# Products of the next heads cut into pieces between the units of two attentions

## The chip, the cores and the metric

The kernel runs on one core of one Trainium2 chip. The metric is the device time of one execution in microseconds (us). Its engines, as the profile names them: PE is TensorE's matmuls, PEld its weight loads, DVE is VectorE, ACT is ScalarE, POOL is GpSimd and SP is SyncE.

## What is computed

A network of two blocks over 512 tokens of width 1024, all in float32. The first block has four layers: a latent attention, a sliding attention, a sparse attention and a latent attention again, each normed, shifted and scaled by a modulation. The second has a hybrid of attention and state space, a short convolution and two gated feed-forward layers. The change touches the two middle layers of the first block:

```python
def swa_mixer(h, positions, w_in, sinks, w_out):
    q, k, v, gate = jnp.split(h @ w_in, ...)            # 16 heads of 64, 2 key heads
    q, k = rope(q), rope(k)
    o = banded_attention(q, k, v, 128, 128, sinks)      # window of 128
    return (o * jax.nn.silu(gate)) @ w_out

def nsa_mixer(h, positions, w_in, cmp_pos, w_cmp_k1, w_cmp_k2, w_cmp_v1, w_cmp_v2, w_out):
    q, k_cmp, v_cmp, k_slc, v_slc, k_win, v_win, g_branch, gate = jnp.split(h @ w_in, ...)
    ...                                                 # 16 heads of 64, 4 key heads
    o = g[..., 0:1] * o_c + g[..., 1:2] * o_s + g[..., 2:3] * o_w
    return (o * jax.nn.silu(gate)) @ w_out
```

`o_c` is attention over 31 compressed blocks, `o_s` over chosen blocks (with 512 tokens all are chosen, so it is causal attention), `o_w` over a window of 512.

## The kernel before

Each engine has its own program, written out by hand, and semaphores join them. An attention runs over units. In the sparse layer (`nsa_units`) a pair of heads has 17: unit 0 is the compressed branch of both heads, units 1 to 8 are the branch of chosen blocks (4 blocks of 128 queries, both heads of each in turn), units 9 to 16 the window; a unit is 128, 256, 384 or 512 keys wide by its query block. There are 8 pairs, so 136 units. In the sliding layer (`swa_units`) a pair has 4 units, one for each query block with both heads.

TensorE's `attend` goes through the steps. At step s it first does what `inserts` holds for s, then the scores of unit s, then it waits for ScalarE's copy of the turned probabilities of unit s-3 and multiplies them with the values (`values`, L1237 and L1226, in the sliding layer L1111; in branches 1 and 2 only after the second head, with both heads' blocks), then it waits for VectorE's normalised probabilities of unit s-2 and turns them (`turn_blocks`, L894) into the one bank PB. VectorE does at step s the row maxima of unit s (L2434; for the compressed branch the three operations L2427 to L2429) and the normalisation of unit s-1 (L2648, L2649). Where VectorE's `inserts` has an entry for the step, the normalisation comes first, then the insert, then the maxima; else the maxima come first. ScalarE does at step s its insert, the copy of the turned unit s-2 (L1754), and the exponential of unit s (L1743).

The inserts make what the next pair needs. `query` and `gate` are products of 8 matmuls of 512 columns (L726), `turn` is one matmul with a rotation table (L726, `psum<-raw,cst`), after which VectorE's `rotate` finishes the rotary embedding. After even pairs the next key head's values are made (`value_tile`, L753), after odd pairs its keys (`key_tile`) and their turn (`key_turn`): ScalarE's part of that waits for VectorE's rotation and makes two copies (L1970, L1971). All go through two PSUM banks by turns: `next_tile` waits until the tile before the last is free, `evacuated` until a tile has been read. Weights come through a ring of two slots (`open_slot`); the load of a slot is issued when the first matmul of the slot before it has run. Query and gate of a pair share a slot. A matmul in float32 is two records in the trace.

`mod_columns(3)` at step 34 sums the columns of GpSimd's job (48 records, L781). `drain_inserts` puts parts of the output projection (L920) into the last steps. The steps at which the products stood, on all three engines: query 2, turn 4, gate 6, next 9, next turn 11 in the sparse layer; query 1, turn 2, gate 3 in the sliding one.

Of the kernel before, what the change touches and what calls it, by code (L numbers as in the profile page):

```python
# [185 lines left out]
NEVER = 3.0e38  # L186
MLA_STEPS = {1: "queries", 2: "keys", 4: "gate 0", 6: "gate 1", 7: "values"}
SWA_STEPS = {1: "query", 2: "turn", 3: "gate"}
NSA_STEPS = {2: "query", 4: "turn", 6: "gate", 9: "next", 11: "next turn"}


def causal_blocks(j):
# [39 lines left out]
def build(nc, A, out, tables, const):  # L232

    ctx = ExitStack()
    with ctx:
# [457 lines left out]
        def _(pe):  # L693
# [382 lines left out]
            def query_tiles(raw_tiles, slots_of):  # L1076
# [10 lines left out]
                    rotated(raw[:, 0, :])  # L1087
                return query, gate, turn

            def swa():  # L1090
                query, gate, turn = query_tiles({}, {})

# [31 lines left out]
                turn(0)  # L1124
                inserts = {}
                for pair in range(7):
                    for at, name in SWA_STEPS.items():
                        part = {"query": query, "gate": gate, "turn": turn}[name]
                        inserts[4 * pair + at] = [lambda part=part, pair=pair: part(pair + 1)]
                attend(swa_units(), scores, turn_blocks, values, inserts={**inserts, **drain_inserts(swa_units())})  # L1130

            def nsa():
# [47 lines left out]
                def value_tile(kv):  # L1180
                    value_tiles[kv] = tokens_tile(open_slot(2), P, range(TT), True)

                key_tile(0)
                slot = open_slot(3)
# [54 lines left out]
                                          stop=(u["branch"] == 2 and i == len(u["blocks"]) - 1), skip_group_check=True)  # L1239
                    return m  # L1240

                inserts = {}
                for pair in range(7):
                    kv = pair // 2 + 1
                    base = 17 * pair
                    inserts[base + 2] = [lambda pair=pair: query(pair + 1)]
                    inserts[base + 4] = [lambda pair=pair: turn(pair + 1)]
                    inserts[base + 6] = [lambda pair=pair: gate(pair + 1)]
                    if pair < 6 and pair % 2 == 0:
                        inserts[base + 9] = [lambda kv=kv: value_tile(kv)]  # L1250
                    if pair < 6 and pair % 2:
                        inserts[base + 9] = [lambda kv=kv: key_tile(kv)]
                        inserts[base + 11] = [lambda kv=kv: key_turn(kv)]
                inserts[17 * 2] = [lambda: mod_columns(3)]
# [426 lines left out]
        def _(act):  # L1681
# [244 lines left out]
            def nsa():  # L1926
# [82 lines left out]
                attend(nsa_units(), -1.0, inserts=inserts)  # L2009

# [238 lines left out]
        def _(dve):  # L2249
# [356 lines left out]
            def nsa():  # L2606
# [78 lines left out]
                for pair in range(7):  # L2685
                    kv = pair // 2 + 1
                    base = 17 * pair
                    inserts[base + 2] = [lambda pair=pair: query(pair + 1)]
                    inserts[base + 4] = [lambda pair=pair: turn(pair + 1)]
                    inserts[base + 6] = [lambda pair=pair: gate(pair + 1)]  # L2690
                    if pair < 6 and pair % 2 == 0:
                        inserts[base + 9] = [lambda kv=kv: value_tile(kv)]
                    if pair < 6 and pair % 2:
                        inserts[base + 9] = [lambda kv=kv: key_tile(kv)]
                        inserts[base + 11] = [lambda kv=kv: key_turn(kv)]
# [540 lines left out]
```

## Time and profile before

| | |
|---|---|
| median of 3 runs | 2867.77 us (2866.61 to 2868.32) |
| the profiled execution | 2861.63 us, its span 2859.8 us |
| mean granted TensorE clock in it | 0.978 |
| TensorE (PE) busy | 2705.7 us, 95% of the span |
| VectorE, ScalarE, GpSimd busy | 1296.1, 655.7, 1072.3 us |
| units of the sliding attention | 367 to 538 us of the span |
| units of the sparse attention | 683 to 1052 us of the span |

The profile is of one execution. A busy TensorE is counted with each matmul's full length, while the next one may start before it ends. In a timeline, idle time and what ended it stand in brackets behind an instruction.

### The profile page before, as it was taken

What the parts mean: (1) busy time and instruction counts of PE and PEld (TensorE: products, weight loads), DVE (VectorE), ACT (ScalarE), POOL (GpSimd) and SP (SyncE); (2) the same over time, 40 slices, a digit from 0 to 9 for tenths busy, and PEclk for the clock granted to TensorE, in tenths of its full rate; (3) what the DMA queues carried; (4) which work ended last, traced back from release to release, by engine and by line L of the source; (5) the groups of instructions that cost most, each with busy time, mean ns of one, the idle gap of its engine ahead of it and who ended that gap; (6) DMA issues with size and microseconds to landing.
All of it is one profiled execution on the core that took longest, in us unless ns stands there. A gap on an engine that the chain in (4) does not pass through costs nothing.

```text
span 2859.8 us, 32196 instructions
## 1 busy us (share of the span) xinstructions
PE 2705.7 (95%) x11791; PEld 1767.7 (62%) x11791; DVE 1296.1 (45%) x2667; ACT 655.7 (23%) x1575; POOL 1072.3 (37%) x574
## 2 busy tenths in 40 slices
PE   6799999998999999999998889899999999999997
PEld 5366544465555554555545665778887444888886
DVE  7133355333655552333555674443554222433554
ACT  2133123232333342322113621111101001111101
POOL 4785188048583003860584001880000880000000
PEclk7899999999999999999999999999999999999999
DMA  7342343145242103331442002442222542222222
GB/s 243 105 133 86 99 130 111 59 122 148 67 119 59 37 30 123 111 98 62 116 134 58 1 16 81 154 155 83 85 92 87 162 159 74 74 83 82 86 91 70
DMA packets 245112, 277.81 MB, mean 97 GB/s; under 512 B 41427, under 2 KB 217824, under 8 KB 244864
## 3 DMA queue, kind: packets, MB, share of 16 engines
q1 hardware_dynamic: 216000, 175.03, 20.2%
q0 software_dynamic: 28224, 100.86, 11.4%
q8 instruction: 78, 1.28, 0.2%
q10 hardware_dynamic: 768, 0.30, 0.0%
q14 instruction: 42, 0.34, 0.0%
HBM read 274.06 MB, written 2.10 MB: 97 GB/s over the span
## 4 chain that ended last, share of the span: by engine, by line
PE 84%; DVE 4%; DMA 3%; ACT 3%; issue 3%; POOL 1%; SPq 1%; DVEq 0%; ACTq 0%; POOLq 0%
PE psum L726 27%; PE psum L1523 25%; PE psum L920 12%; PE psum L894 3%; PE psum L1219 2%; PE psum L781 2%; PE psum L1237 1%; PE psum L906 1%; DMA ring<-in_ffn_w_gate 1%; PE psum L1059 1%; PE psum L1060 1%; PE psum L753 1%; PE psum L1354 1%; DMA ring<-in_ffn_w_up 1%; POOL ada_ring L668 1%
## 5 line engine op out<-in xcount | busy, mean ns | idle before, releaser
L726 PE MATMUL psum<-h,ring 128*128 128x512 f32 (+1 forms) x1776 | 758.9, 585 | 15.3 <-ACT arena L1704 4.7
L656 POOL DMA_DIRECT2D ada_ring<-in_ada_w x192 | 114.7, 597 | 1266.0 <-DVEq L2336 796.0
L726 PEld LDWEIGHTS psum<-h,ring 128*128 128x128 f32 x1776 | 335.7, 192 | 399.5 <-issue 381.9
L668 POOL TENSOR_SCALAR ada_ring<-ada_ring,cond 128x1024 f32<-128x1024 f32 x168 | 480.5, 2860 | 8.4 <-POOL ada_sum L672 2.1
L672 POOL TENSOR_TENSOR ada_sum<-ada_sum,ada_ring 128x1024 f32<-128x1024 f32 x168 | 398.6, 2373 | 14.9
L920 PE MATMUL psum<-og,ring 128*128 128x512 f32 x768 | 333.3, 593 | 0.3
L1523 PE MATMUL psum<-og,arena 128*128 128x256 f32 x1152 | 258.6, 379 | 1.7 <-ACT probs L2160 1.7
L920 PEld LDWEIGHTS psum<-og,ring 128*128 128x128 f32 x768 | 144.5, 190 | 179.1 <-issue 179.1
L1523 PEld LDWEIGHTS psum<-og,arena 128*128 128x128 f32 x1152 | 218.7, 190 | 32.1 <-issue 2.4
L1523 PE MATMUL psum<-h,ring 128*128 128x256 f32 x768 | 177.7, 382 | 1.6 <-DVE mods L2334 0.9
L1754 ACT ACTIVATE probsT<-psum 128x128 f32<-128x128 f32 (+3 forms) x232 | 104.3, 450 | 293.9 <-PE psum L894 293.2
L1523 PEld LDWEIGHTS psum<-h,ring 128*128 128x128 f32 x768 | 145.7, 191 | 25.9 <-ACT h L1719 5.1
L1787 ACT ACTIVATE sq<-x 128x512 f32<-128x512 f32 x63 | 39.7, 630 | 424.7 <-DVE x L2500 228.5
L2160 ACT ACTIVATE probs<-psum 128x256 f32<-128x256 f32 x132 | 50.7, 384 | 373.1 <-PE psum L1523 373.1
L3036 DVE SCALAR_TENSOR_TENSOR x<-psum,mods,x 128x256 f32<-128x256 f32 x168 | 81.1, 483 | 112.1 <-PE psum L1523 110.8
L894 PE MATMUL psum<-cst,arena 128*128 128x128 f32 x608 | 112.3, 286 | 20.2 <-ACT probsT L1754 10.8
L2500 DVE SCALAR_TENSOR_TENSOR x<-psum,mods,x 128x512 f32<-128x512 f32 x48 | 36.0, 751 | 204.3 <-PE psum L920 203.9
L1743 ACT ACTIVATE psum<-psum,neg_max 128x256 f32<-128x256 f32 (+3 forms) x256 | 122.1, 477 | 26.4 <-DVE neg_max L2434 26.1
L2434 DVE CUSTOM_DVE_ANT_0 psum<-psum,cst 128x128 f32<-128x128 f32 (+1 forms) x192 | 94.5, 499 | 72.4 <-PE psum L1060 33.6
L1704 ACT ACTIVATE arena<-psum 128x512 f32<-128x512 f32 (+4 forms) x100 | 55.0, 557 | 281.2 <-PE psum L726 228.0
L1523 PE MATMUL psum<-og,ring 128*128 128x256 f32 x400 | 98.9, 391 | 17.8 <-DVE arena L3010 17.8
L1523 PE MATMUL psum<-h,arena 128*128 128x256 f32 x480 | 113.4, 379 | 0.0
(383 smaller groups left out, 3578.0 us busy)
## 6 DMA issues: line engine op xcount, KB each, us to landing
ada_ring<-in_ada_w POOLq DMA_DIRECT2D x192, 512.0 KB, 4.1
ring<-in_ffn_w_gate SPq DMA_DIRECT2D x22, 1024.0 KB, 5.4
ring<-in_ffn_w_up SPq DMA_DIRECT2D x22, 1024.0 KB, 5.3
ring<-in_ffn_w_down SPq DMA_DIRECT2D x16, 1024.0 KB, 5.1
ring<-in_sc_w_in SPq DMA_DIRECT2D x12, 1024.0 KB, 6.0
ring<-in_mla_w_in SPq DMA_DIRECT2D x10, 1024.0 KB, 5.4
ring<-in_mla_w_out SPq DMA_DIRECT2D x8, 1024.0 KB, 5.2
ring<-in_swa_w_in SPq DMA_DIRECT2D x16, 512.0 KB, 5.4
```

The costliest lines, as they stand in the source:

```text
L656: pool.dma_start(ada_ring[:, i % 2, :], w[k * P:(k + 1) * P, first(part)]).then_inc(arrived[i % 2], n.give(f"ada_in{i % 2}", 16))
L668: step = nc.gpsimd.tensor_scalar(piece, ada_ring[:, i % 2, :], c, None, ALU.mult)
L672: step = nc.gpsimd.tensor_tensor(total, total, piece, ALU.add)
L726: m = pe.matmul(tile.at[:, part], lhs(k), rhs(k), start=(k == 0), stop=(k == K - 1))
L781: m = pe.matmul(tile.at[:, c:c + width], ada_sum[:, c * P:(c + 1) * P], ones[:, 0:width], start=True, stop=True)
L894: m = pe.transpose(bank[:, i * P:(i + 1) * P], p[:, block_at:block_at + P], ident)
L920: m = pe.matmul(out_tiles[c].at, w8(out_slots[0], P * (c % 2))(k), og[:, k * T:(k + 1) * T], start=(k == 0), stop=(k == KT - 1))
L1523: last = pe.matmul(out, weights[:, k, :], moving[:, k, :], start=begins and k == 0, stop=True, skip_group_check=True)
L1743: e = nc.scalar.activation(scored, scored, ACT.Exp, bias=neg_max[:, step % 4, g:g + 1], scale=scale, accum_out=row_sum[:, step % 4, g:g + 1])
L1754: c = nc.scalar.activation(probsT[:, i % 2, 0:w], PB[:, 0:w], ACT.Copy)
L2434: last = nc.vector.tensor_tensor_reduce(s[:, at:at + w], s[:, at:at + w], mask(u), -scale, floor, ALU.add, ALU.min, neg_max[:, b, g:g + 1])
L3036: nc.vector.scalar_tensor_tensor(xq, bank, scales[q], xq, ALU.mult, ALU.add).then_inc(S[told], n.give(told))
```

## The change

In the sparse layer TensorE's query, gate and next products are cut into pieces of one to three matmuls (`NSA_PIECES`), one piece a step, so that the last piece stands at the step of `NSA_STEPS`. Query: steps 0, 1, 2. Turn: 4. Gate: 4 to 8. Next keys or values: 9 to 13. Next turn: 15. VectorE's and ScalarE's parts stand at the steps of the last pieces, so gate goes from 6 to 8, next from 9 to 13, next turn from 11 to 15. In the sliding layer TensorE's query is cut four and four over steps 0 and 1, its gate four and four over steps 2 and 3; the other engines' steps stay. `pieces` and `value_pieces` are new functions; they issue the same matmuls in the same order within a product.

```diff
-NSA_STEPS = {2: "query", 4: "turn", 6: "gate", 9: "next", 11: "next turn"}
+NSA_STEPS = {2: "query", 4: "turn", 8: "gate", 13: "next", 15: "next turn"}
+NSA_PIECES = {"query": (3, 3, 2), "gate": (1, 1, 2, 2, 2), "next": (2, 2, 1, 1, 2)}
...
+            def pieces(sizes, weights, slot_of=None):
+                made, out, at = {}, [], 0
+                def piece(first, size):
+                    if first == 0:
+                        if slot_of is not None:
+                            made["slot"] = slot_of()
+                        made["tile"] = next_tile()
+                    for k in range(first, first + size):
+                        m = pe.matmul(made["tile"].at, weights(made)(k), h_lat(k), start=(k == 0), stop=(k == KT - 1))
+                        if k == 0 and slot_of is not None:
+                            m.then_inc(S["slot_begun"], n.give("slot_begun"))
+                    if first + size == KT:
+                        m.then_inc(S["tile_done"], 1)
+                for size in sizes:
+                    out.append(lambda at=at, size=size: piece(at, size))
+                    at += size
+                return out, made
+
+            def value_pieces(sizes, tiles, kv):
+                made, out, at = {}, [], 0
+                def piece(first, size):
+                    if first == 0:
+                        made["slot"] = open_slot(2)
+                        tiles[kv] = next_tile()
+                    for i in range(first, first + size):
+                        j, half = i // 2, i % 2
+                        for k in range(4 * half, 4 * half + 4):
+                            m = pe.matmul(tiles[kv].at[:, j * P:(j + 1) * P], h[:, k, j * P:(j + 1) * P],
+                                          w8(made["slot"], 0)(k), start=(k == 0), stop=(k == KT - 1))
...
             def swa():
...
-                    for at, name in SWA_STEPS.items():
-                        part = {"query": query, "gate": gate, "turn": turn}[name]
-                        inserts[4 * pair + at] = [lambda part=part, pair=pair: part(pair + 1)]
+                    base = 4 * pair
+                    asked, made = pieces((4, 4), lambda m: w8(m["slot"], 0), lambda: open_slot(2))
+                    gated, _ = pieces((4, 4), lambda _, made=made: w8(made["slot"], P))
+                    def turned(made=made):
+                        evacuated(made["tile"])
+                        rotated(raw[:, 0, :])
+                    for at, part in enumerate([[asked[0]], [asked[1]], [turned, gated[0]], [gated[1]]]):
+                        inserts[base + at] = part
...
             def nsa():
...
-                inserts = {}
+                inserts = {step: [] for step in range(17 * 8)}
+                inserts[17 * 2].append(lambda: mod_columns(3))
+                def spread_over(last, parts, base):
+                    for i, part in enumerate(parts):
+                        inserts[base + last + 1 - len(parts) + i].append(part)
...
-                    inserts[base + 2] = [lambda pair=pair: query(pair + 1)]
-                    inserts[base + 4] = [lambda pair=pair: turn(pair + 1)]
-                    inserts[base + 6] = [lambda pair=pair: gate(pair + 1)]
+                    spread_over(at["query"], asked, base)
+                    spread_over(at["turn"], [turned], base)
+                    spread_over(at["gate"], gated, base)
                     if pair < 6 and pair % 2 == 0:
-                        inserts[base + 9] = [lambda kv=kv: value_tile(kv)]
+                        spread_over(at["next"], value_pieces(NSA_PIECES["next"], value_tiles, kv), base)
                     if pair < 6 and pair % 2:
-                        inserts[base + 9] = [lambda kv=kv: key_tile(kv)]
-                        inserts[base + 11] = [lambda kv=kv: key_turn(kv)]
+                        keyed, key_made = pieces(NSA_PIECES["next"], lambda m: w8(m["slot"], 0), lambda: open_slot(2))
+                        def keys_turned(key_made=key_made):
+                            evacuated(key_made["tile"])
+                            rotated(raw[:, 0, :])
+                        spread_over(at["next"], keyed, base)
+                        spread_over(at["next turn"], [keys_turned], base)
...
 # on ScalarE and on VectorE alike
-                    inserts[base + 6] = [lambda pair=pair: gate(pair + 1)]
+                    inserts[base + 8] = [lambda pair=pair: gate(pair + 1)]
                     if pair < 6 and pair % 2 == 0:
-                        inserts[base + 9] = [lambda kv=kv: value_tile(kv)]
+                        inserts[base + 13] = [lambda kv=kv: value_tile(kv)]
                     if pair < 6 and pair % 2:
-                        inserts[base + 9] = [lambda kv=kv: key_tile(kv)]
-                        inserts[base + 11] = [lambda kv=kv: key_turn(kv)]
+                        inserts[base + 13] = [lambda kv=kv: key_tile(kv)]
+                        inserts[base + 15] = [lambda kv=kv: key_turn(kv)]
```

## Rows read from the trace of the kernel before

**Rows 1.** Stretches of both attentions and of one clock dip (busy by engine, clock, DMA).

```profile
367.00:526.00 159.00, 156.22 (x595) 74.29 (x596) 92.86 (x281) 56.47 (x214) 111.23 (x58) 1.00 0.38 109
683.00:1052.00 369.00, 346.12 (x1907) 205.70 (x1908) 214.19 (x629) 139.82 (x421) 150.97 (x78) 0.99 0.24 69
869.00:875.00 6.00, 4.29 (x14) 2.29 (x15) 3.29 (x12) 3.76 (x12) 5.57 (x4) 0.72 0.31 86
```

**Rows 2.** TensorE's waits, 684 to 1052: us in total, times, longest.

```profile
PE psum L894 <- ACT probsT L1754: 10.8, 12, 2.2
PE psum L894 <- DVE arena L2649: 7.1, 6, 1.2
PE psum L1237 <- ACT probsT L1754: 3.0, 9, 0.6
```

**Rows 3.** TensorE's timeline, pair 1 of the sparse attention: start, us, instruction, count, idle before.

```profile
728.20 0.39 PE L1219 MATMUL psum<-arena 128*128 128x128 f32 x2
729.78 0.63 PE L894 MATMUL psum<-cst,arena 128*128 128x128 f32 x4 [1.20 <-DVE arena L2649]
...
743.26 7.03 PE L726 MATMUL psum<-h,ring 128*128 128x512 f32 x16
750.13 0.81 PE L1219 MATMUL psum<-arena 128*128 128x384 f32 x2
...
750.99 1.02 PE L1219 MATMUL psum<-arena 128*128 128x512 f32 x2
751.95 0.66 PE L1237 MATMUL psum<-probsT,arena 128*64 128x128 f32 x8
...
752.92 1.02 PE L1219 MATMUL psum<-arena 128*128 128x512 f32 x2
754.01 0.52 PE L894 MATMUL psum<-cst,arena 128*128 128x128 f32 x3
...
763.70 0.66 PE L894 MATMUL psum<-cst,arena 128*128 128x128 f32 x4 [0.46 <-ACT probsT L1754]
764.19 1.02 PE L726 MATMUL psum<-raw,cst 128*128 128x512 f32 x2
...
766.77 0.60 PE L1219 MATMUL psum<-arena 128*128 128x256 f32 x2
769.58 0.33 PE L894 MATMUL psum<-cst,arena 128*128 128x128 f32 x1 [2.21 <-ACT probsT L1754]
...
771.22 0.81 PE L1219 MATMUL psum<-arena 128*128 128x384 f32 x2
772.17 0.41 PE L894 MATMUL psum<-cst,arena 128*128 128x128 f32 x2
```

**Rows 4.** TensorE's timeline: a value product in sliding pair 1, one in sparse pair 0.

```profile
387.85 0.66 PE L1111 MATMUL psum<-probsT,arena 128*64 128x128 f32 x8 [0.25 <-ACT probsT L1754]
...
718.41 1.09 PE L1237 MATMUL psum<-probsT,arena 128*64 128x128 f32 x16 [0.25 <-ACT probsT L1754]
```

**Rows 5.** TensorE's timeline, last steps of the sliding attention.

```profile
530.88 2.74 PE L920 MATMUL psum<-og,ring 128*128 128x512 f32 x6
533.55 0.66 PE L1111 MATMUL psum<-probsT,arena 128*64 128x128 f32 x8
```

**Rows 6.** Timeline of VectorE and TensorE where the sparse units start.

```profile
681.15 0.69 DVE L2408 SCALAR_TENSOR_TENSOR arena<-arena,psum 128x512 f32<-128x512 f32 x1 [6.18 <-ACT arena L1726]
...
683.28 1.10 PE L1215 MATMUL psum<-arena 128*128 128x64 f32 x8 [2.02 <-DVEq L2389]
```

**Rows 7.** ScalarE's timeline at the key turn of pair 1.

```profile
768.10 0.63 ACT L1970 ACTIVATE arena<-arena 64x512 f32<-64x512 f32 x1 [2.76 <-DVEq L2389]
...
769.27 0.25 ACT L1754 ACTIVATE probsT<-psum 128x128 f32<-128x128 f32 x1
```

**Rows 8.** Loads of queries and gates: count, KB, us to landing.

```profile
ring<-in_nsa_w_in SPq DMA_DIRECT2D x16, 512.0 KB, 5.1
```

**Rows 9.** GpSimd's timeline after the column sums of step 34.

```profile
781.77 0.61 POOL L656 DMA_DIRECT2D ada_ring<-in_ada_w  x1 [26.90 <-DVE gains L2310]
```

More of the change, by code:

```diff
@@ L1088, in query_tiles @@
                 return query, gate, turn
+            def pieces(sizes, weights, slot_of=None):
[26 more added lines that the diff above has]
+                                          w8(made["slot"], 0)(k), start=(k == 0), stop=(k == KT - 1))
+                            if i == 0 and k == 0:
+                                m.then_inc(S["slot_begun"], n.give("slot_begun"))
+                    if first + size == 2 * TT:
+                        m.then_inc(S["tile_done"], 1)
+                for size in sizes:
+                    out.append(lambda at=at, size=size: piece(at, size))
+                    at += size
+                return out
             def swa():
@@ L1178, in key_turn @@
                     rotated(raw[:, 0, :])
-                def value_tile(kv):
-                    value_tiles[kv] = tokens_tile(open_slot(2), P, range(TT), True)
                 key_tile(0)
@@ L1245, in nsa, with turned @@
                     base = 17 * pair
-                    inserts[base + 2] = [lambda pair=pair: query(pair + 1)]
-                    inserts[base + 4] = [lambda pair=pair: turn(pair + 1)]
-                    inserts[base + 6] = [lambda pair=pair: gate(pair + 1)]
+                    at = {name: step for step, name in NSA_STEPS.items()}
+                    asked, made = pieces(NSA_PIECES["query"], lambda m: w8(m["slot"], 0), lambda: open_slot(2))
+                    gated, _ = pieces(NSA_PIECES["gate"], lambda _, made=made: w8(made["slot"], P))
+                    def turned(made=made):
+                        evacuated(made["tile"])
+                        rotated(raw[:, 0, :])
+                    spread_over(at["query"], asked, base)
+                    spread_over(at["turn"], [turned], base)
+                    spread_over(at["gate"], gated, base)
                     if pair < 6 and pair % 2 == 0:
-                        inserts[base + 9] = [lambda kv=kv: value_tile(kv)]
+                        spread_over(at["next"], value_pieces(NSA_PIECES["next"], value_tiles, kv), base)
                     if pair < 6 and pair % 2:
-                        inserts[base + 9] = [lambda kv=kv: key_tile(kv)]
-                        inserts[base + 11] = [lambda kv=kv: key_turn(kv)]
-                inserts[17 * 2] = [lambda: mod_columns(3)]
+                        keyed, key_made = pieces(NSA_PIECES["next"], lambda m: w8(m["slot"], 0), lambda: open_slot(2))
+                        def keys_turned(key_made=key_made):
+                            evacuated(key_made["tile"])
+                            rotated(raw[:, 0, :])
+                        spread_over(at["next"], keyed, base)
+                        spread_over(at["next turn"], [keys_turned], base)
                 attend(nsa_units(), scores, turn_blocks, values, inserts={**inserts, **drain_inserts(nsa_units())})
@@ L2689, in nsa @@
                     inserts[base + 4] = [lambda pair=pair: turn(pair + 1)]
-                    inserts[base + 6] = [lambda pair=pair: gate(pair + 1)]
+                    inserts[base + 8] = [lambda pair=pair: gate(pair + 1)]
                     if pair < 6 and pair % 2 == 0:
-                        inserts[base + 9] = [lambda kv=kv: value_tile(kv)]
+                        inserts[base + 13] = [lambda kv=kv: value_tile(kv)]
                     if pair < 6 and pair % 2:
-                        inserts[base + 9] = [lambda kv=kv: key_tile(kv)]
-                        inserts[base + 11] = [lambda kv=kv: key_turn(kv)]
+                        inserts[base + 13] = [lambda kv=kv: key_tile(kv)]
+                        inserts[base + 15] = [lambda kv=kv: key_turn(kv)]
                 inserts[17 * 2] = [lambda: mod_columns(3, col("norm_g", 24, 8))]
```

## The prediction

> **What bounds the kernel now.** I read the page first (the table above): TensorE is busy 95% of the span, so the time can only fall by work that leaves TensorE (none does: the change moves products and removes none) or by stalls that leave it. Then the two stages that the change touches, as stretches: in the sliding attention TensorE is busy 156.2 of 159 us, in the sparse attention 346.1 of 369 us, at granted clocks of 1.00 and 0.99 [rows 1]. So the sparse stage holds some 23 us of idle time and the sliding one 3. Then who ended these waits: ScalarE's copies of turned probabilities and VectorE's normalised ones, 10.8, 7.1 and 3.0, together 20.9 us in 27 waits, none over 2.2 us [rows 2]. They are latencies of the hand-over between the engines, not a full engine: VectorE is busy 214 and ScalarE 140 of the 369 us [rows 1]. Last the timeline of one pair of heads [rows 3], which shows where in the 17 steps they stand.
>
> How [rows 3] must be read: a recorded matmul is longer than the time until the next may start. A product of 16 records starts at 743.26 and the scores after it at 750.13: 6.87 us, 0.43 for each record of 512 columns, recorded as 0.59; in proportion 0.32, 0.22 and 0.11 us for 384, 256 and 128 columns. A true stall is thus the start minus the end by these spacings, some 0.16 us more than the idle time in brackets, and there are stalls with no bracket. The stalls of a pair, its branch-0 unit being step 0:
> - step 1: scores at 728.20 take 0.22, the turning starts at 729.78: 1.36 us. VectorE first does the three maxima operations of the compressed branch, then the normalisation that is waited for. Six times: pairs 1, 3, 5 and 6 as here, pair 4 with 0.14 less, pair 2 only 0.62 (idle 0.46): 7.3 us together.
> - step 8: 752.92 + 0.86 = 753.78, next start 754.01: 0.23 us, in seven pairs.
> - step 10: idle 0.46 before 763.70, so 0.62 us, in eight pairs; it is the copy of four turned blocks that must leave the one bank.
> - step 11 of pairs with no key turn there: idle 0.25 at 718.41, some 0.32 us over what such a start costs anyway (0.09) [rows 4].
> - step 12 of pairs 1, 3 and 5: scores at 766.77 take 0.44, the turning starts at 769.58: 2.37 us.
> - step 14: 771.22 + 0.65 = 771.87, next start 772.17: 0.30 us, in eight pairs.
>
> **What the change does, part by part.** *Cutting products up.* Per pair the query goes 3, 3 and 2 matmuls at steps 0 to 2 (it was 8 at step 2), the gate 1, 1, 2, 2, 2 at steps 4 to 8 (8 at step 6), the next keys or values in five pieces at steps 9 to 13 (all at 9); the key turn goes from 11 to 15. That adds 2 x 7 + 4 x 7 + 4 x 6 = 66 interruptions of an accumulation in the sparse stage and 14 in the sliding one, 80 together. Their price: a turning of four blocks starts at 763.70 and a product with the rotation table at 764.19, four spacings of 0.11 and 0.05 later; at 750.13 the scores follow a product at its own spacing [rows 3]. The output projection's accumulation is already interrupted in the sliding stage's last steps: six records start at 530.88, the values at 533.55, which is 6 x 0.43 + 0.09 [rows 5], and 0.10 is what a start of values costs behind scores too (750.99 + 0.86, then 751.95 [rows 3]). I take 0 per interruption; the upper end is 0.1 us, 8 us in all; no row suggests a gain.
>
> *Cover.* One matmul is two records, 0.86 us; pieces of 1, 2 and 3 are 0.86, 1.71 and 2.57 us. Each stall is a chain on other engines that runs on while TensorE works, so a piece between its start and its end takes it away up to the piece's length. Step 1 gets 2.57 us between scores(0) and the awaited turning, against 1.36: gone in pairs 1 to 6, 7.3 us. Step 8 gets 1.71 against 0.23: seven times, 1.6 us. Step 10 gets 1.71 or so against 0.62 in the six pairs with a next product: 3.7 us. Step 11, 0.86 against 0.32 in pairs 0, 2, 4: 1.0 us. Step 14 gets no piece, but VectorE now has an entry at step 13 and so normalises unit 12 before the maxima of 13, and not after: the 0.30 goes in six pairs, 1.7 us (bounds 0 and 1.7). Pair 7 has no products and keeps its stalls; pair 6 has no next product and keeps steps 9 to 11 (some 1.1 us of idle time).
>
> *Start of each attention.* Scores of pair 0 wait 2.02 us of idle time, 2.17 by spacing, for VectorE's rotation. Now the first piece stands ahead of them. It needs the bank that VectorE's gate product frees at 681.15 + 0.69 = 681.84, 0.73 us after the rotating matmul is through (683.28 - 2.17); it ends at 681.95 + 2.57 = 684.5, after the rotation. Scores then start at 684.5, where before scores and the same 2.57 us would have been through 683.28 + 2.57 = 685.85: 1.3 us saved [rows 6]. The sliding stage starts in the same way (the same 2.02 us of idle time): 1.3 us more.
>
> *The key turn.* ScalarE's part of it waits for VectorE's rotation, then makes two copies, and only then copies the turned block that TensorE waits for: it stands idle 2.76 us until 768.10, copies to 769.27, then takes the block, and TensorE goes on at 769.58 [rows 3, 7]. From 764.14, the end of the turning before it, the chain is 5.4 us, and TensorE has 3.0 us of work beside it. Moved to step 15 the chain has the same members. From the turning of step 14: copy 0.5 and exp 0.7, normalising 0.8, rotation 2.1, copies 1.2, block 0.4, with hand-overs some 5.9 us; TensorE has rotation 0.86, scores 0.86, values 0.66, turning 0.33, scores 0.86, together 3.6. The stall moves to step 16 with 2.3 us; if VectorE is still behind from taking the keys at step 13, 2.6. No piece stands at step 16, and those of the next step 0 come behind the wait. So 2.4 three times is given back as 2.4 or 2.5: cost 0.3 us in all (bounds: 3 us better, 2 us worse). Queued behind it is the turning of step 16; the next scores come 2.6 us later, which hides the late exp and normalisation.
>
> *What gets less cover.* In pair 0 the compressed unit's turning at step 2 has 1.7 + 0.2 us after scores(1), and VectorE takes maxima 0.3 and weighing 1.8 first: 0.7 us new. Pair 6's gate now ends at step 8, VectorE's and ScalarE's work on it stands right before the uncovered steps 9 and 10: 0.3 us new. Elsewhere the chains (1.5 to 3.9 us) lie under 4 to 6 us of TensorE work. VectorE's operations are sometimes stretched beside GpSimd; I leave up to 2 us for that.
>
> *Sliding attention.* The query goes 4 and 4 at steps 0 and 1, the gate 4 and 4 at 2 and 3. At each step 0 a value product waits 0.25 us (387.85) [rows 4], 0.32 by spacing; six of these steps now get 3.43 us ahead of them, 1.9 us, and one turning of pair 0 saves 0.2. VectorE's and ScalarE's steps don't move there.
>
> *Loads.* A slot's load starts with the first matmul of the slot before. The query is now opened two steps earlier, but still eight steps after its load starts, and the loads land in 5.1 us [rows 8]; TensorE's waits name none [rows 2]. GpSimd's job that the column sums of step 34 read was through at 754.9, for GpSimd then stands idle 26.90 us for what comes of these sums [rows 9], so they may come 10 us earlier.
>
> **The sum.** Sparse: 7.3 + 1.6 + 3.7 + 1.0 + 1.7 + 1.3 - 0.3 - 0.7 - 0.3 = 15.3 us. Sliding: 1.3 + 1.9 + 0.2 = 3.4. Together 18.7 us. The profiled execution took 2861.6 (span 2859.8), it would take 2843; the median of the runs is 6.1 higher, and there I take off the same: 2867.8 - 18.7 = 2849.
>
> **The clock.** Two dips fall in the sparse stage, each 6 us at 0.72 on average, so 1.7 us lost, and both follow a key-turn stall [rows 1] (the other at 968 to 974); pair 1 has the same stall and no dip. As that stall stays, I keep both; 3.4 us is the most that can be won. The Trainium skill ("TensorE: Matmul & The Clock Gate", A second HAM failure mode: psum-queue depth-cycling) says that matmul groups which go round the PSUM banks leave TensorE idle so briefly and so often that its clock swings between the two levels. By that rule the cut products would cost clock. This trace disagrees: the sliding stage changes bank every 1 to 3 us and is granted 1.00.
>
> **Rivals.**
> 1. *As forecast*, 12 to 23 us saved: 0.70.
> 2. *The stalls come back elsewhere*: the chain of each unit is late at the small pieces (0.86 us) or behind the key turn, or interruptions cost near 0.1 us. Half the gain, 6 to 12 us: about 2858. For it: steps 14 to 16 have no piece. Against: pair 7, with no pieces at all, has only 3.3 us of idle time. 0.16.
> 3. *Nothing to be measured*: the piece boundaries cost 0.2 us, as each start of a value product costs 0.09 and some of the compressed branch's 0.2: 80 x 0.2 = 16, leaving 3 us: about 2865. 0.08.
> 4. *Slower*: an interrupted accumulation costs a start of its own. From 0.29 us per interruption, 80 of which are 23 us, the kernel is over 0.2% slower; at 0.35 it is 28 - 18.7 = 9 us slower, 2877. Against it: [rows 5]. 0.02.
> 5. *Clock swings*, the skill's rule as a mechanism of this kernel: a dip in each of 14 pairs instead of 2, 12 x 1.7 = 20 us: 2869, no change. Against: the sliding stage's 1.00 with two dozen changes of bank a pair [rows 1]. 0.04 (of which half slower).
>
> **Numbers.** What a measurement tells from no change is 0.2%, 5.7 us. Faster: 0.86 (cases 1 and 2); within: 0.10; slower: 0.04. The range must hold 8 in 10: case 1 from 23 us (both dips and part of the key turn gone: 2844) and case 2 to about 9 us: 2859.
>
> **What would show it.** Right: TensorE's waits in the sparse stage fall from 21 us to some 10, namely three of 2.2 to 2.5 us behind the key turn, now at step 16, and the rest in pairs 6 and 7; no 1.20 at step 1 except in pair 7; the stage, 369 us, is some 15 shorter with the same busy time; spacing at piece ends 0.11 and 0.43. The start waits of 2.02 shrink to about 0.7 or turn into one for the bank. Wrong: spacings over 0.5 us at piece ends (cases 3, 4), new waits at steps 4 to 8 or of more than 3 us at 16 (case 2), a granted clock below 0.98 (case 5). It would also be wrong if the key turn's stall vanished: then some 7 us more.

## The result, and the profile after

The changed kernel took 2846.48 us (median of 6 runs, 2840.47 to 2853.9), the kernel before 2867.35 us (6 runs, 2858.96 to 2869.29). The ratio is 0.993 with an interval of 0.9912 to 0.9948: some 20 us less, between 15 and 25. The forecast was 2849 us and 18.7 us less.

The profiled execution took 2844.35 us, 17.3 less than the one before; its span is 2842.5. On the page TensorE is busy 95% of the span as before (2705.7 us then), and its granted clock has the same tenths:

```profile
PE 2699.3 (95%) x11791; PEld 1768.6 (62%) x11791; DVE 1314.0 (46%) x2667; ACT 659.5 (23%) x1575; POOL 1069.4 (38%) x574
...
PEclk7899999999999999999999999999999999999999
```

The windows of the two attentions, from the rotating matmul ahead of the first unit to where the output projection goes on after the last values (before: 364.29 to 538.75 and 680.25 to 1051.77), and of two clock dips (columns as in [rows 1]):

```profile
363.46:538.84 175.38, 170.74 (x655) 80.87 (x653) 114.82 (x301) 64.43 (x234) 112.91 (x58) 0.99 0.35 105
677.67:1031.20 353.53, 340.48 (x1909) 206.12 (x1908) 215.01 (x630) 143.96 (x423) 155.73 (x81) 1.00 0.26 74
527.00:533.00 6.00, 4.87 (x17) 2.60 (x18) 2.86 (x12) 2.47 (x8) 0.00 (x0) 0.72 0.09 16
766.00:772.00 6.00, 4.35 (x24) 4.35 (x25) 3.40 (x8) 3.42 (x8) 0.00 (x0) 0.72 0.01 1
```

The sparse attention is 353.5 us long where it was 371.5: 18.0 less. One dip of the clock lies in it (at 768, behind the key turn of pair 1) where there were two, which is 1.7 us of that; the stalls are the other 16.3. The sliding attention is 175.4 us where it was 174.5, with a dip at 529 that was not there (1.7 us): at equal clock it is 0.8 less, and 3.4 were forecast. What lies outside both made 0.2 us: 0.8 less ahead of them, 2.7 less between them, where the clock dips cost 5.1 us before and 1.7 now, and 3.3 more behind them, in code that the change doesn't touch. Single executions differ by that much.

TensorE's waits of the sparse stage, which answer to [rows 2] (L895 turns blocks, L1285 multiplies with values, L1101 is a piece of a product, L2714 normalises):

```profile
PE psum L895 <- ACT probsT L1819: 7.0, 4, 2.2
PE psum L1285 <- ACT probsT L1819: 2.3, 6, 0.6
PE psum L895 <- DVE arena L2714: 1.8, 2, 1.2
PE psum L1101 <- DVE arena L2473: 0.7, 1, 0.7
PE psum L895 <- DVE arena L2723: 0.5, 1, 0.5
```

Together these are 11.6 us beside the 0.7 at the first piece; before it was 20.9. The timeline shows where, by the readings of [rows 3, 6]:

```profile
677.67 1.02 PE L727 MATMUL psum<-raw,cst 128*128 128x512 f32 x2
679.42 2.81 PE L1101 MATMUL psum<-h,ring 128*128 128x512 f32 x6 [0.72 <-DVE arena L2473]
682.07 1.00 PE L1263 MATMUL psum<-arena 128*128 128x64 f32 x8
...
688.38 0.44 PE L895 MATMUL psum<-cst,arena 128*128 128x128 f32 x2 [0.52 <-DVE arena L2723]
...
728.59 0.39 PE L1267 MATMUL psum<-arena 128*128 128x128 f32 x2
728.81 0.60 PE L895 MATMUL psum<-cst,arena 128*128 128x128 f32 x4
...
764.44 1.02 PE L1267 MATMUL psum<-arena 128*128 128x512 f32 x2
767.65 0.56 PE L895 MATMUL psum<-cst,arena 128*128 128x128 f32 x3 [2.19 <-ACT probsT L1819]
```

The first piece waits 0.72 us for the bank of the gate tile and the first scores start at 682.07; those wait for nothing. In pair 1 the turning follows the scores of step 1 at 0.22 us, the bare spacing, where it stood 1.36 us. At step 16 it stands 2.19 us by the row, 767.65 - 764.44 - 0.86 = 2.35 by spacing. ScalarE's rows are those of [rows 7], four steps later:

```profile
765.95 0.63 ACT L2035 ACTIVATE arena<-arena 64x512 f32<-64x512 f32 x1 [3.02 <-DVEq L2454]
...
767.13 0.47 ACT L1819 ACTIVATE probsT<-psum 128x384 f32<-128x384 f32 x1
```

In the sliding stage the 0.25 us waits of [rows 4] are gone from pairs 1 to 6 and the 2.02 us at its start are 0.72. But the first row here is new: before, TensorE waited 0.5 us once ahead of the rotating matmul (L727), for the query to be taken:

```profile
PE psum L727 <- DVE tmp L2441: 2.0, 3, 0.9
PE psum L1156 <- ACT probsT L1819: 0.9, 2, 0.7
```

The reason is on VectorE. It has the same 301 instructions and is busy 114.8 us, not 99.9. One line makes the difference, the sum of `row_sum` and `sink_exp`, 128x2 elements. Its row before:

```profile
L2448 DVE TENSOR_TENSOR row_sum<-row_sum,sink_exp 128x2 f32<-128x2 f32 x32 | 13.6, 426 | 28.0 <-ACT psum L1743 27.9
```

and after:

```profile
L2513 DVE TENSOR_TENSOR row_sum<-row_sum,sink_exp 128x2 f32<-128x2 f32 x32 | 30.2, 944 | 24.1 <-ACT psum L1808 24.0
```

From 426 to 944 ns on average with single ones of 2351 ns, as long as GpSimd's sums take. It is not so in every execution, as the experiments show below. The timeline at pair 1 (GpSimd, VectorE and TensorE) shows what is behind it:

```profile
389.82 2.34 POOL L673 TENSOR_TENSOR ada_sum<-ada_sum,ada_ring 128x1024 f32<-128x1024 f32 x1
...
389.83 2.35 DVE L2513 TENSOR_TENSOR row_sum<-row_sum,sink_exp 128x2 f32<-128x2 f32 x1
...
393.21 1.46 DVE L2513 TENSOR_TENSOR row_sum<-row_sum,sink_exp 128x2 f32<-128x2 f32 x1
...
393.69 1.02 PE L1144 MATMUL psum<-arena 128*128 128x512 f32 x2
...
395.42 0.68 DVE L2440 COPY raw<-psum 128x512 f32<-128x512 f32 x1
...
396.76 0.70 PE L727 MATMUL psum<-raw,cst 128*128 128x512 f32 x1 [0.87 <-DVE tmp L2441]
```

The query is through at 393.7 us, but VectorE starts to take it at 395.42, behind two normalisations whose sums took 2.35 and 1.46 us, and TensorE's rotating matmul waits 0.87 us. The first of these sums starts 0.01 us behind a sum of GpSimd and ends with it. The second (393.21 to 394.67) ends with no instruction of GpSimd; what stretched it isn't shown.

### The profile page after: what moved, and what is told of

Its sections match the earlier page's. It is cut to its first block, busy times and chain, and to the rows that moved or that the text cites. A ratio compares the mean times of both kernels' runs of the same rounds, so it can differ in the third digit from the quotient of the medians.

```text
span 2842.5 us, 32196 instructions
## 1 busy us (share of the span) xinstructions
PE 2699.3 (95%) x11791; PEld 1768.6 (62%) x11791; DVE 1314.0 (46%) x2667; ACT 659.5 (23%) x1575; POOL 1069.4 (38%) x574
## 4 chain that ended last, share of the span: by engine, by line
PE 86%; DVE 4%; DMA 3%; ACT 2%; issue 2%; POOL 1%; SPq 1%; DVEq 0%; ACTq 0%; POOLq 0%
PE psum L1588 27%; PE psum L727 20%; PE psum L921 12%; PE psum L1101 7%; PE psum L895 3%; PE psum L1267 2%; PE psum L782 2%; PE psum L1285 1%; PE psum L907 1%; PE psum L1060 1%; PE psum L1061 1%; PE psum L1419 1%; PE psum L1123 1%; DMA ring<-in_ffn_w_gate 1%; POOL ada_ring L669 1%
## 5 line engine op out<-in xcount | busy, mean ns | idle before, releaser
L657 POOL DMA_DIRECT2D ada_ring<-in_ada_w x192 | 114.8, 598 | 1251.9 <-DVEq L2401 803.6
L727 PE MATMUL psum<-h,ring 128*128 128x512 f32 (+1 forms) x1280 | 538.9, 580 | 16.2 <-DVE arena L2345 4.7
L727 PEld LDWEIGHTS psum<-h,ring 128*128 128x128 f32 x1280 | 243.1, 192 | 295.4 <-issue 277.0
L1101 PE MATMUL psum<-h,ring 128*128 128x512 f32 x496 | 229.4, 593 | 1.4 <-DVE arena L2473 1.4
L1101 PEld LDWEIGHTS psum<-h,ring 128*128 128x128 f32 x496 | 87.8, 191 | 81.8 <-issue 81.0
L895 PE MATMUL psum<-cst,arena 128*128 128x128 f32 x608 | 110.9, 284 | 10.6 <-ACT probsT L1819 7.0
```

The lines of the kernel that those rows point to most:

```text
L657: pool.dma_start(ada_ring[:, i % 2, :], w[k * P:(k + 1) * P, first(part)]).then_inc(arrived[i % 2], n.give(f"ada_in{i % 2}", 16))
L727: m = pe.matmul(tile.at[:, part], lhs(k), rhs(k), start=(k == 0), stop=(k == K - 1))
L895: m = pe.transpose(bank[:, i * P:(i + 1) * P], p[:, block_at:block_at + P], ident)
L1101: m = pe.matmul(made["tile"].at, weights(made)(k), h_lat(k), start=(k == 0), stop=(k == KT - 1))
```

## The experiments

Times of a kernel come with the ratio to the kernel before on the same chip. Stage lengths and stalls are read from one profiled execution of each; the sparse stage is given from its first scores to its last values (368.3 us before, 348.9 in the changed kernel), and a stall by spacing. In the changed kernel the query's first piece, 2.57 us, stands ahead of the first scores and so outside this length; before, the whole query lay inside. The lengths therefore compare kernels that have this piece, and the 18.0 us above compare the change with the kernel before.

**The two layers apart.** One kernel has the sliding layer's edit alone, one the sparse layer's alone; the other layer's code is that of before.

> The sliding layer's cut alone, the sparse layer as before. My theory (cover of stalls at each step 0 and at the start): 3.4 us faster than before, so 2864, within 0.2% of it; in the profile the waits of 0.25 us at step 0 of pairs 1 to 6 are gone and the 2.02 us at the start has become 0.7. Rival (the sliding layer brings nothing, its products only go elsewhere): the same waits at other steps, 2867. Rival (an interruption costs 0.3 us or more): 14 of them, slower by 4.

2866.69 us against 2866.48, ratio 0.9987 (0.997 to 1.0004): no gain that can be told from none. The waits of 0.25 us are gone, and 2.04 us stand at one rotating matmul of pair 0, with a clock dip right behind it (376 to 380, 1.7 us). The rival that stalls change place is nearer than mine.

> The sparse layer's part alone, the sliding layer as before. My theory: 15 to 17 us faster than before, about 2851, with three waits of 2.2 us left at step 16 of pairs 1, 3 and 5. Rival (the two layers share the gain evenly): 2857.

2844.13 us, ratio 0.9915 (0.989 to 0.9939). The whole measured gain is here, with a stage of 350.3 us and two clock dips in it. The interval, 17 to 32 us, lies at and above my 15 to 17. The three waits of 2.2 us at step 16 are there as said.

**Moved and not cut.**

```diff
-NSA_PIECES = {"query": (3, 3, 2), "gate": (1, 1, 2, 2, 2), "next": (2, 2, 1, 1, 2)}
+NSA_PIECES = {"query": (8,), "gate": (8,), "next": (8,)}
```

> The steps of the sparse layer moved as in the change (gate 8, next 13, key turn 15), but each product in one piece of 8, and the sliding layer as before. My theory (cutting is what pays, since a cover is worth something only at the step where a chain runs out): the stalls of step 1 stay (7.3 us), those of 8 and 14 go (3.3 us), and steps 6, 9, 10 and 11 lose the cover they had, some 6 to 7 us, so 3 us slower than before, 2870, within 0.2%. Rival (the gain comes from the later steps and the earlier normalisation, not from the cutting): 10 us or more faster, 2855.

2879.9 us, ratio 1.005 (1.0036 to 1.0063): 14 us slower than before. The moves alone cost, and the rival that they are the gain is out. My 3 us were too few by a stall that the kernel before never shows, since its gate stood on it: behind the rotation of step 4, VectorE is late with unit 4, and the turning of step 6 waits. The scores at 744.47 take 0.65, the turning starts at 746.92, 1.80 us later, in seven pairs, 12.6 us:

```profile
744.47 0.81 PE L1261 MATMUL psum<-arena 128*128 128x384 f32 x2
746.92 0.41 PE L895 MATMUL psum<-cst,arena 128*128 128x128 f32 x2 [1.64 <-DVE arena L2708]
...
PE psum L895 <- DVE arena L2708: 21.6, 19, 1.6
```

**Is an interruption free?** Each piece of the changed kernel is halved, and the second half goes behind the scores.

```diff
+                        piece(at, size - size // 2)
+                        if size // 2:
+                            behind.append(lambda: piece(at + size - size // 2, size // 2))
...
```

> The changed kernel, but of every piece of 2, 3 or 4 matmuls the later half (rounded down) is put behind the scores of its step: some 88 interruptions more, the same work in each step. My theory (an interruption costs nothing): as the changed kernel within 2 us, 2846 to 2849, spacings 0.43 and 0.11 at the new ends. Rival (an interruption costs 0.1 us, and the change would have won 8 us more without them): 9 us slower than the changed kernel, 2856.

2846.19 us, ratio 0.9924 (0.9902 to 0.9946), as the changed kernel. In the timeline a piece (L1105), the scores (L1279), the other half and the values follow one another at 0.87, 0.22, 0.86 + 0.09 us:

```profile
732.35 0.60 PE L899 MATMUL psum<-cst,arena 128*128 128x128 f32 x4
732.78 1.02 PE L1105 MATMUL psum<-h,ring 128*128 128x512 f32 x2
733.65 0.38 PE L1279 MATMUL psum<-arena 128*128 128x128 f32 x2
733.87 1.02 PE L1105 MATMUL psum<-h,ring 128*128 128x512 f32 x2
734.82 1.09 PE L1297 MATMUL psum<-probsT,arena 128*64 128x128 f32 x16
```

The 88 more interruptions show no cost in the times of the runs. By their intervals alone up to some 0.07 us each could hide there; it is the spacings that show the bare rate. In the profile, the sliding stage is 1.8 us longer at equal clock, with waits at seven rotating matmuls, since the query's last half now comes behind the scores. The sparse stage is 3.3 us longer: the key turn's three stalls are 2.99 us and not 2.35, pair 6 stands 0.7 longer at step 10, both because the last half ends later; that leaves under 1 us for the 60 interruptions there.

**The key turn.** ScalarE's part goes behind the copy that TensorE waits for. VectorE's stays at 15.

```diff
-                        inserts[base + 15] = [lambda kv=kv: key_turn(kv)]
+                        inserts[base + 16] = [lambda kv=kv: key_turn(kv)]
```

> The changed kernel with one edit: ScalarE's part of the key turn (wait for the rotation, two copies) stands at its step 16 and not 15, so behind the copy of the turned unit 13 and the exponential of 15. My theory (the stall of 2.35 us at step 16 is that copy, queued behind a wait for VectorE's rotation): the three stalls go, 7 us less than the changed kernel, about 2840; at most 1 us comes back at the next pair's first steps. Rival (VectorE is late itself: behind the rotation stand the maxima and normalisation of 15, so the wait only changes its name): within 2 us of the changed kernel, with a wait for VectorE at step 16 or 0.

2840.23 us, ratio 0.9902 (0.9884 to 0.9919), 6 us less than the changed kernel, whose interval overlaps. The profile is clearer: the stage is 342.1 us, 6.8 less, of which 1.7 is the clock dip of the changed kernel that has no counterpart here, and the turning of step 16 follows its scores at the bare 0.86 us: three stalls of 2.35 us are gone. Of these, 1.5 us of idle time came back at the first scores of pairs 4 and 6 (L1263), which now wait for the copies themselves:

```profile
766.28 1.02 PE L1267 MATMUL psum<-arena 128*128 128x512 f32 x2
767.14 0.49 PE L895 MATMUL psum<-cst,arena 128*128 128x128 f32 x3
...
PE psum L1263 <- ACT arena L2036: 1.5, 2, 0.7
```

**Few pieces.** Two pieces a product; the query at 1 and 2, the gate at 7 and 8, the next one at 9 and 10.

```diff
+NSA_PIECES = {"query": (4, 4), "gate": (4, 4), "next": (4, 4)}
...
-                        spread_over(at["next"], keyed, base)
+                        spread_over(at["next"] - 3, keyed, base)
...
```

> The changed kernel with two pieces of 4 for each product of the sparse layer instead of three or five: query at steps 1 and 2, gate at 7 and 8, keys or values at 9 and 10; all later steps of the other engines as in the change. My theory (what counts is that some piece stands at a step where a chain runs out): step 1, 8, 9 and 10 stay covered; step 11 loses its cover (0.32 us in six pairs, 1.9 us), step 12 0.1, and behind the query's rotation at step 4 nothing stands at 5 and 6, where the uncut gate's absence cost 1.8 us in seven pairs in the kernel with moved, uncut products: 12.6 us. Sum 15 us slower than the changed kernel, about 2861. Rival (the number of pieces matters, small ones being better as such): the 15 us would be spread over all steps and not stand at step 6.

2869.32 us, ratio 1.0007 (0.9994 to 1.002): all of the gain is lost, 23 us against the changed kernel where I had said 15. Step 6 stands 1.80 us in each of seven pairs again, step 11 0.32 in all. Not foreseen: 0.76 us ahead of each key turn, since no piece stands at 13 while VectorE takes the keys, 0.64 more at the three stalls of step 16 and 0.25 in the even pairs, 1.2 us at the start, where no piece stands at step 0 now (scores wait 2.02 us again), and three clock dips in the stage, one of them double: 13.6 us at the lower level, so 6.8 us lost where the one dip of the changed kernel costs 1.7.

```profile
PE psum L895 <- DVE arena L2714: 13.3, 9, 1.6
PE psum L895 <- ACT probsT L1819: 8.9, 4, 2.8
```

Nearly the same number of pieces, better placed: the gate's two at steps 5 and 6, the query's two kept, the next product in three (3, 3, 2) at 9, 10 and 11.

```diff
+NSA_PIECES = {"query": (4, 4), "gate": (4, 4), "next": (3, 3, 2)}
...
-                    spread_over(at["gate"], gated, base)
+                    spread_over(at["gate"] - 2, gated, base)
...
```

> As the kernel with pieces of four, other steps: gate 4 and 4 at steps 5 and 6 (not 7 and 8), next product 3, 3, 2 at 9, 10, 11; what the other engines do stands at 8, 13 and 15 as in the change. My theory (a piece is worth something where a chain runs out, and behind the query's rotation that is step 6): the 1.8 us at step 6 of seven pairs and the 0.32 at step 11 go, 0.23 at step 8 comes, so some 13 us less than with pieces of four, about 2855; against the changed kernel it keeps what stands at 8, 14 and 16. Rival (pieces must be small): no better than pieces of four, 2869.

2855.3 us, ratio 0.9967 (0.9953 to 0.9981): 14 us less by the medians than the pieces of four before it, as said (11 by the ratios). Step 6 is free of stalls in the seven pairs. That small pieces are worth something as such is out; the place decides. It is still 9 us above the changed kernel. What it lacks to it is the start (2.02 us, for step 0 has no piece), the 0.76 us ahead of each key turn, step 16 (2.98 us three times, 0.25 in the even pairs), 1.1 more at step 10 of pair 6 and 0.11 at step 8. Step 14, where I had expected a stall, has none in pairs 0 to 5.

**The sliding layer.** The rotating matmul and the gate's first piece stand behind the scores of step 2.

> The changed kernel, but in the sliding layer the rotating matmul and the gate's first piece stand behind the scores of step 2 and not ahead of them. My theory (the new waits ahead of the rotating matmul, 0.7 to 1.05 us in pairs 0, 1, 3 and 5, are VectorE's taking of the query, which now runs behind a normalisation that the query's first piece has delayed): scores of 0.86 us cover most of them, the sliding stage is 1.5 to 2.3 us shorter at equal clock. Rival (the wait is for the bank of the tile, however late): it stays in full.

One run: 2844.0 us. The stage, from the rotating matmul to the last values, takes 170.1 us; it took 174.3 before and 175.2 (173.5 without the dip) in the changed kernel. The waits ahead of the rotating matmul are gone, and what is left is the 0.72 us for the bank at the start and the waits of the last pair's drain. The sum's operations, 682 ns on average here, no longer reach TensorE. At equal clock that is 3.4 us less than the changed kernel's profile, more than I had said; but that profile is one with long sums, as the table below shows, and against the best one of the same sliding code it is 0.7.

And the sum itself, in the changed kernel:

```diff
-                        settle(nc.vector.tensor_tensor(row_sum[:, b, 0:G], row_sum[:, b, 0:G], sink_exp[:, b, 0:G],
-                                                       ALU.add))
+                        for g in range(G):
+                            added = nc.vector.tensor_scalar(row_sum[:, b, g:g + 1], row_sum[:, b, g:g + 1],
+                                                            sink_exp[:, b, g:g + 1], None, ALU.add)
+                        settle(added)
```

> The changed kernel; in the sliding layer VectorE's sum of row_sum and sink_exp (128x2, both in SBUF, 32 times) is two operations of 128x1 with sink_exp as a column scalar. Its mean grew from 426 to 944 ns with the change, 16.6 us in all, with single ones of up to 2351 ns, which is as long as a sum of GpSimd. My theory (it waits for GpSimd's operation, and that wait stands ahead of the taking of the query): the two operations take about 0.15 us each, VectorE's busy time in the sliding stage falls by some 20 us, the new waits ahead of the rotating matmul shrink from 2.0 us of idle time to under 0.8, and the sliding stage is 1.5 to 2 us shorter. Rival (the late taking is from the order normalisation, then query, and not from GpSimd): VectorE's busy time falls, the waits ahead of the rotating matmul stay.

2844.18 us, ratio 0.9923 (0.9896 to 0.995): not told apart by the runs. By the profile: twice as many operations, 209 ns each (202 to 215), 10.7 us in place of 30.2; TensorE waits 0.5 us for the query as before the change, and the stage is 171.2 us.

```profile
L2514 DVE TENSOR_SCALAR row_sum<-row_sum,sink_exp 128x1 f32<-128x1 f32 x64 | 10.7, 209 | 27.9 <-ACT psum L1808 27.9
...
PE psum L727 <- DVE tmp L2441: 0.5, 1, 0.5
```

That alone doesn't show what the sum costs the change, for several of the other kernels have the very same sliding code as the changed one, and their profiled executions differ. Line, mean of the 128x2 sum, TensorE's waits at the rotating matmul, and the stage to the last values, 1.7 us a clock dip taken off:

| kernel | sum, ns | waits, us | stage, us |
|---|---|---|---|
| before (old code) | 426 | 0.5 | 174.3 |
| changed | 944 | 2.0 | 173.5 |
| sliding layer alone | 868 | 2.2 | 173.1 |
| key copies later | 864 | 2.1 | 172.9 |
| few pieces, well placed | 638 | 1.2 | 172.4 |
| pieces of four | 442 | 0.5 | 170.8 |
| changed, sum by column scalar | 209 | 0.5 | 171.2 |

Stage and waits follow the sum, but for small differences. In the execution where the sums stayed as short as before, the sliding change saved 3.5 us, and with the rewritten sum 3.0. In two of these executions (sliding layer alone, key copies later) the first rotating matmul waits some 2 us and a clock dip follows at once, at 376 and 377 us. The table takes such dips off. If they come from the stall, it understates its cost by 1.7 us each; two cases don't show that they do.

**Together.** Key copies later, the sliding turn behind the scores, and the products of the last pair of the sparse layer spread over the last two pairs.

> Three edits on the changed kernel: ScalarE's key copies at 16, the sliding layer's turn behind the scores, and in the sparse layer's last two pairs the products of pair 7 spread over both (query over steps 1 to 11 of pair 6 with its turn at 13, gate over steps 1 to 14 of pair 7), so that the stalls of both pairs are covered. My theory: 7 + 2 + 5.5 = 14.5 us less than the changed kernel, about 2832. Rival (what is taken away comes back behind it): half of it, 2839.

2839.76 us, ratio 0.991 (0.9892 to 0.9928): the rival's half, and not told apart from the key copies alone. Two of my edits met. The first scores of pair 6 wait for the key copies, now made late, and I had taken the query's piece from in front of them; and the turn at 13 had nothing behind it:

```profile
952.09 1.08 PE L1267 MATMUL psum<-arena 128*128 128x64 f32 x8 [3.31 <-ACT arena L2053]
...
PE psum L1289 <- ACT probsT L1836: 1.7, 2, 1.1
```

> As the kernel with all three edits, but pair 8's products spread otherwise: query 3 and 2 at steps 0 and 1 of the pair before the last, one each at 2, 8 and 9, its turn at 10, the gate one each at 11 and 12 and 2, 1, 1, 1, 1 at steps 1, 2, 9, 10 and 11 of the last pair. My theory (there the scores of step 0, which wait for the key copies, had no piece in front and stood 3.5 us, and the turn at 13 had nothing behind it, 1.2 us): both go, and of the last two pairs' stalls only those of steps 6 and 14 and the drain stay, so 5 us less than with the key copies alone, and 3.4 us from the sliding layer: about 2832. Rival (the last pairs' stalls only change place, as with all three before): 2837.

2835.72 us, ratio 0.9903 (0.9886 to 0.992). That is nearer to the rival's 2837 than to my 2832, and by its ratio no faster than the key copies alone (0.9902). In the profile both new stalls are gone and the stage is 338.2 us, 10.7 less than in the changed kernel (9.0 at equal clock); 1.26 us stand ahead of the turn at step 10 of pair 6.

> The kernel with all three edits mended, and the same edit of the sum. My theory: there only one wait of 1.1 us ahead of the rotating matmul is left, so 0.5 to 1 us less, about 2835. Rival: more, if the wait for GpSimd also delayed other units: up to 2 us, 2833.

2829.59 us (5 runs, 2828.07 to 2833.59), ratio 0.987 (0.9847 to 0.9894): the fastest of all, 37 us less than before and by its interval apart from the changed kernel, but not from the kernel without the last edit. It is also below what I (2835) and the rival (2833) had said. Its profile has a sparse stage of 338.2 us with these waits left of 20.9 us:

```profile
PE psum L1267 <- ACT arena L2053: 1.5, 2, 0.7
PE psum L727 <- DVE tmp L2463: 1.1, 1, 1.1
PE psum L1289 <- ACT probsT L1836: 0.6, 1, 0.6
```

The two stages are within 1 us of the kernel without the last edit, so they don't explain the 6 us between the medians. Of the 5.0 us between the profiled executions, 3.6 lie ahead of the sliding stage (it starts at 361.47 and not at 365.03), where the two programs are the same. The last edit is thus not shown to be worth more than 1 us.

## Why the prediction was right

- *What bounds it*: right. TensorE's work stayed, its waits fell, the time fell by them. 18.7 us forecast, 20 (15 to 25) measured. The two stages of the profile account for 17.1 of them at equal clock, one a little above its forecast and one well below; that the total comes so near to 18.7 is in part that the two misses offset each other.
- *Cover in the sparse stage*: 15.3 us forecast, 16.3 in the profile at equal clock. Term by term, by spacing: step 1 7.3 us gone as said, pair 7 keeps its 1.37; step 8 1.6 gone; step 10 3.8 gone of 3.7 and 0.81 in pair 6 in place of 0.62 (0.3 said, 0.2 found); step 11 1.0 gone; step 14 1.7 gone in pairs 0 to 5, by the earlier normalisation; pair 0's step 2 0.69 new (0.7 said). The start saved 1.2: from the rotating matmul to the scores it was 3.03 us with no piece and is 4.40 with one of 2.57.
- *Key turn*: 2.3 to 2.6 us at step 16 forecast, 2.35 found in each. That it is a matter of ScalarE's order is shown by moving that alone.
- *An interruption costs nothing*: shown by the spacings at the ends of the pieces, and nothing in the times of 88 more of them speaks against it.
- *Sliding layer*: 3.4 us forecast, 0.8 found in the changed kernel's profile. The parts named were saved (1.9 at step 0, 1.2 at the start), and some 2 came back. The step that failed is "VectorE's and ScalarE's steps don't move there": true of the program and not of the time. With short sums the same code saves 3.5 us, the forecast; in four of the five profiled executions of it the sums were stretched and it saved 0.8 to 1.9. In three of the old code (before, sparse layer alone, uncut) they stayed at 387 to 449 ns. That the new order makes it likelier is suggested by this and not shown, with five executions against three; what decides between executions stays open. I had allowed 2 us for VectorE's stretched operations, in the other stage, and put none of it into the sum.
- *The clock*: I had kept two dips in the sparse stage; one fell there and one in the sliding stage. The mechanism of the fifth rival didn't show: with 80 more interruptions, and with 88 more still, the stages of this and the doubled kernel were granted 0.99 to 1.00. By that, the rule of the Trainium skill ("TensorE: Matmul & The Clock Gate", A second HAM failure mode: psum-queue depth-cycling) is not seen here.
- What the sum couldn't see, as the experiment with uncut products showed: that the cover of step 6 in the kernel before hid 1.8 us a pair. The change is right there because its gate pieces stand at 4, 5 and 6, which I had argued only in general, by chains of up to 3.9 us under 4 to 6 us of work.

## What to carry to other kernels

When one engine is nearly full and its waits are short hand-overs, list them by step, and put movable work between the start and the end of each, as long as the chain is late: a product of 6.9 us at one step covers a stall of 1.8 there and leaves five others open. Look also for the stall that today's cover hides, before moving it. Then look at what a piece delays: the same scores that now come later start somebody's chain, and work taken from one place (the first scores of a pair) can be the cover of the next edit.

## What the runs showed of the hardware

- A sum of 128x2 elements on VectorE, both inputs in SBUF, has a median of 161 ns in the kernel before and of 1040 in the changed one, up to 2351, beside GpSimd's sums of 2.34 us, and differs by execution with the same code; written with a column scalar it is two operations of 209 ns, none over 215. The Trainium skill ("SBUF — State Buffer", Who interferes with whom) says that a VectorE operation with two SBUF inputs reads the second one through an interface that it shares with GpSimd, and that this shared pair of ports is an exclusive lock. The rows at 389.8 us agree: the longest sum, 2.35 us, lasts as long as one sum of GpSimd and ends with it. The sum of 1.46 us behind it ends with none, which that section doesn't explain here.
- An accumulation on TensorE may be left and taken up again, with scores, values and transpositions into other banks between, at the bare spacing: 0.43 us for each record of 512 columns.
- The dips of the granted clock (1.7 us each) come in places that differ from one execution to the next, with the same code of a stage: in the sliding stage of the new order one at 529 us in the changed kernel, two (at 376 and 529) with the key copies later, none with the pieces of four. So the dips of one profile are taken off before stages are compared.
